# Causal masks added by VectorE, head outputs split in pairs, rotated queries moved by transfers, in a two-layer decoder trunk

## The reference, cut to what matters

```python
D_MODEL = 1024; SEQ = 512; DEPTH = 2          # batch 1
HEAD_DIM = 64; N_HEADS = 16; NSA_GROUPS = 4   # 4 query heads share one key/value group

def nsa_mixer(x, ...):                        # layer 0
    q, kc, vc, ks, vs, kw, vw, gl = split(x @ w_in)
    gates = sigmoid(gl + b_gate)              # three gates for each head and token
    q_rot, k_slc, k_win = apply_rope(q), apply_rope(ks), apply_rope(kw)
    k_cmp, v_cmp = compress(kc, ...), compress(vc, ...)      # 31 compressed keys per group
    # compressed branch: unrotated q, key n seen if 16 n + 31 <= t; rows that see none give 0
    # selected branch: n_sel = min(16, 8) = 8 of 8 blocks, so all of the causal keys
    # window branch: the last 512 positions, so all of the causal keys too
    return (g0 * softmax(q k_cmp) v_cmp + g1 * softmax(q_rot k_slc) v_slc
            + g2 * softmax(q_rot k_win) v_win) @ w_o

def fox_mixer(x, ...):                        # layer 1
    q, k, v, fl = split(x @ w_in)
    cum = cumsum(log_sigmoid(fl + b_f))
    return softmax_causal(q k / 8 + cum_q - cum_k) v @ w_o

def conv_ffn(x, ...):
    h = causal_conv3(x @ w_up) + conv_b
    a, b = split(h)
    return (gelu(a) * b) @ w_down

for i in range(2):
    x = layer_norm(ALPHA * x + mixer_i(x))
    x = layer_norm(ALPHA * x + conv_ffn(x))
```

## Time and profile before

| | us |
|---|---|
| median of 3 runs (lowest, highest) | 1415.19 (1414.56, 1415.60) |
| profiled execution, its own time | 1415.75 |
| its span, first to last instruction | 1414.0 |
| TensorE (PE) busy | 1355.5 |
| VectorE (DVE) busy | 700.9 |
| ScalarE (ACT) busy | 671.1 |
| GpSimd (POOL) busy | 618.3 |

### The profile page before, as it was taken

One profiled execution on the slowest core, in us unless ns is written; L12 is line 12 of the kernel. 1 busy time (PEld: TensorE's weight loads), 2 busy tenths in 40 slices (PEclk: granted clock), 3 DMA queues, 4 the chain that ended last, 5 costly groups with the idle time before them and its releaser, 6 DMA issues.

```text
span 1414.0 us, 20012 instructions
## 1 busy us (share of the span) xinstructions
PE 1355.5 (96%) x7050; PEld 1116.4 (79%) x7050; DVE 700.9 (50%) x1312; ACT 671.1 (47%) x1249; POOL 618.3 (44%) x406
## 2 busy tenths in 40 slices
PE   8979999988999999999999999998999999999997
PEld 6867787867888888888888778877788888888886
DVE  3347777786554434340007578778374343432006
ACT  4347777776234444442213667777234444443110
POOL 2257777673345444444434222223235444444441
PEclk9989999999999999999999999999999999999999
DMA  9432222111333333333232221222423333334221
GB/s 286 100 75 53 45 60 61 54 38 48 124 96 106 97 96 91 102 100 129 99 89 92 69 75 47 66 72 75 149 60 105 104 93 100 89 104 134 91 74 59
DMA packets 170237, 127.59 MB, mean 90 GB/s; under 512 B 24032, under 2 KB 155860, under 8 KB 170164
## 3 DMA queue, kind: packets, MB, share of 16 engines
q1 hardware_dynamic: 170164, 126.63, 30.5%
HBM read 116.98 MB, written 4.39 MB: 86 GB/s over the span
## 4 chain that ended last, share of the span: by engine, by line
PE 78%; DVE 13%; issue 3%; ACT 3%; POOL 2%; DMA 1%; SPq 1%; DVEq 0%; POOLq 0%; ACTq 0%
PE ps L927 15%; PE ps L929 15%; PE ps L928 15%; PE ps L1185 7%; PE ps L1187 6%; PE ps L1184 6%; PE ps L1089 2%; DVE xt L1606 2%; PE ps L1103 2%; PE ps L1056 2%; DVE prob L1463 1%; DVE xt L1596 1%; DVE negmax L1450 1%; DVE stats L1600 1%; PE ps L1225 1%
## 5 line engine op out<-in xcount | busy, mean ns | idle before, releaser
L466 POOL TENSOR_TENSOR wl<-raw,wh 128x1024 fp32r<-128x1024 f32 x178 | 432.7, 2434 | 667.7 <-ACT wh L585 667.6
L927 PE MATMUL ps<-xh,wh 128*128 128x512 f32 x968 | 392.2, 405 | 1.6 <-ACT work L657 1.0
L929 PE MATMUL ps<-xh,wl 128*128 128x512 f32 x968 | 378.9, 391 | 0.0
L928 PE MATMUL ps<-xl,wh 128*128 128x512 f32 x968 | 378.0, 391 | 0.0
L585 ACT ACTIVATE wh<-raw 128x1024 fp32r<-128x1024 f32 x192 | 201.9, 1052 | 201.1 <-PE ps L1187 190.9
L929 PEld LDWEIGHTS ps<-xh,wl 128*128 128x128 f32 x968 | 182.2, 188 | 39.1
L927 PEld LDWEIGHTS ps<-xh,wh 128*128 128x128 f32 x968 | 184.1, 190 | 34.7 <-ACT work L657 1.4
L928 PEld LDWEIGHTS ps<-xl,wh 128*128 128x128 f32 x968 | 182.9, 189 | 32.1
L1627 DVE SCALAR_TENSOR_TENSOR work<-ps,conv,work 128x511 f32<-128x511 f32 x88 | 66.0, 750 | 221.2 <-ACT work L807 155.8
L1596 DVE SCALAR_TENSOR_TENSOR xt<-xt,ps 128x512 f32<-128x512 f32 x32 | 20.5, 682 | 242.7 <-PE ps L1187 242.4
L1185 PE MATMUL ps<-wl,gh 128*128 128x512 f32 x352 | 139.6, 396 | 0.0
(11 more groups left out here) (198 smaller groups left out, 2076.6 us busy)
## 6 DMA issues: line engine op xcount, KB each, us to landing
raw<-in_ffn_w_up SPq DMA_DIRECT2D x88, 512.0 KB, 3.8
raw<-in_ffn_w_down SPq DMA_DIRECT2D x44, 512.0 KB, 3.5
raw<-in_fox_w_in SPq DMA_DIRECT2D x24, 512.0 KB, 4.0
raw<-in_nsa_w_in SPq DMA_DIRECT2D x12, 512.0 KB, 5.5
xt<-in_x SPq DMA_DIRECT2D x8, 512.0 KB, 4.8
raw<-in_nsa_w_in SPq DMA_DIRECT2D x16, 256.0 KB, 3.9
raw<-in_nsa_w_o SPq DMA_DIRECT2D x8, 512.0 KB, 3.8
raw<-in_fox_w_o SPq DMA_DIRECT2D x8, 512.0 KB, 3.5
```

The costliest lines, as they stand in the source:

```text
L466: nc.gpsimd.tensor_tensor(wl[:, slot, :, :], raw[:, slot, :, :], wh[:, slot, :, :].bitcast(F32), ALU.subtract).then_inc(s_wl, 1)
L927: nc.tensor.matmul(o, ah, bh, start=start, stop=False)
L928: nc.tensor.matmul(o, ah, bl, start=False, stop=False)
L929: return nc.tensor.matmul(o, al, bh, start=False, stop=stop)
```

## The change

- The bf16 mask product is gone. `unit_max` is now one instruction that adds the scores (PSUM) and a bf16 tile `seen` [128, 512] (zeros, then the triangle), writes the negated sum to `prob` and accumulates the minimum, which is the negated maximum. It is followed by an instruction that reads the accumulator out. ScalarE takes the exponential from `prob` with scale -1, in place, and no longer from PSUM; TensorE's wait for a free bank of scores is now for that VectorE instruction.
- `head_add` puts two heads into the two halves of `head_sum`, and `heads_hi` and `heads_lo` split 128 partitions once for two heads: 16 of each in place of 32. The copied half goes to `extra`, or to `swapped` in layer 1.
- The hi part of a query item goes to `swapped` and its lo part to `rot2`, each as one operation of 128 partitions. Four transfers of 64 partitions (`move_queries`) take them to `qs`. The next swap and the next sine product wait for them, and so does TensorE before the first scores that use them.
- The sine product stands at w = 1 in place of 2, ScalarE's hi part of queries at w = 2 in place of 3.
- Two small VectorE floors in the compressed branch are gone (L1493, L1502). Before the units begin, the gates of the first 128 tokens are multiplied once by 0 for tokens without a compressed key. `pcs` has one buffer in place of two.

```diff
-            def mask(bank, i, stop=True):
-                return nc.tensor.matmul(ps[:, bank, i * P:(i + 1) * P], identb[:, :], causalb[:, :], start=False, stop=stop)
             def nsa_scores(u):
...
                     pe.wait_ge(s_pl, 4 * g + 3 + h // 2)
+                    pe.wait_ge(s_qm, 64 * (2 * g + 1 + h // 2))
...
                 if u >= 2:
-                    pe.wait_ge(s_ex, u - 1)
+                    pe.wait_ge(s_nm, u - 1)
                 for part in range(2):
-                    nc.tensor.matmul(..., start=part == 0, stop=False)
-                mask(b, i).then_inc(s_sc, 1)
+                    last = nc.tensor.matmul(..., start=part == 0, stop=part == 1)
+                last.then_inc(s_sc, 1)
...
             def unit_max(u, i):
                 dve.wait_ge(s_sc, u + 1)
-                nc.vector.tensor_reduce(negmax[:, u % 4:u % 4 + 1], ps[:, BS + u % 2, 0:(i + 1) * P], AX.X, ALU.max, negate=True).then_inc(s_nm, 1)
+                if u >= 3:
+                    dve.wait_ge(s_pt, u - 2)
+                n = (i + 1) * P
+                nc.vector.tensor_tensor_reduce(out=prob[:, u % 3, 0:n], in0=ps[:, BS + u % 2, 0:n], in1=seen[:, SEQ - n:SEQ], scale=-1.0, scalar=3e38,
+                                               op0=ALU.add, op1=ALU.min, accum_out=negmax[:, u % 4:u % 4 + 1]).then_inc(s_nm, 1)
...
             def unit_exp(u, i):
                 act.wait_ge(s_nm, u + 1)
-                if u >= 3:
-                    act.wait_ge(s_pt, u - 2)
-                nc.scalar.activation(prob[:, u % 3, 0:n], ps[:, BS + u % 2, 0:n], ACT.Exp,
-                                     bias=negmax[:, b:b + 1], accum_out=psumrow[:, b:b + 1]).then_inc(s_ex, 1)
+                nc.scalar.activation(prob[:, u % 3, 0:n], prob[:, u % 3, 0:n], ACT.Exp,
+                                     bias=negmax[:, b:b + 1], scale=-1.0, accum_out=psumrow[:, b:b + 1]).then_inc(s_ex, 1)
...
+            def move_queries(n):
+                q = qs[n // 4 % 2]
+                a = 2 * (n % 4 - 2)
+                sp.wait_ge(s_ph, n + 1)
+                for h, rows in enumerate(halves):
+                    sp.dma_start(q[rows, a + h, :].bitcast(F32), swapped[rows, :]).then_inc(s_qm, 16)
+                sp.wait_ge(s_pl, n + 1)
+                for h, rows in enumerate(halves):
+                    sp.dma_start(q[halves[1 - h], a + h, :].bitcast(F32), rot2[rows, :]).then_inc(s_qm, 16)
             def item_moves(n):
+                if n % 4 == 3 or n % 4 == 0 and n:
+                    move_queries(n - 1)
...
             def item_hi(g, k):
                     act.wait_ge(s_r3, n - (n + 2) // 4 + 1)
+                    if k:
+                        nc.scalar.activation(swapped.bitcast(F32R), rot1, ACT.Copy).then_inc(s_ph, 1)
+                        return
...
-                    if turned and w == (5 if item[1] == 1 else 3):
+                    if turned and w == (3, 5, 2, 2)[item[1]]:
                         item_hi(*item)
...
-                    if turned and w == (6 if item[1] == 1 else 2):
+                    if turned and w == (6 if item[1] == 1 else 1):
                         item_dve(*item)
...
             def head_add(n, bank):
-                nc.vector.tensor_tensor(head_sum[HD:P, :], ps[0:HD, bank, :], head_sum[0:HD, :], ALU.add).then_inc(s_os, 1)
+                x = extra if n < HEADS else swapped[0:HD, :]
+                nc.vector.tensor_tensor(head_sum[n % 2 * HD:(n % 2 + 1) * HD, :], ps[0:HD, bank, :], x[:, :], ALU.add).then_inc(s_os, 1)
-            def head_lo(n, o_h, o_l):
+            def heads_lo(n, o_h, o_l):
                 dve.wait_ge(s_oh, n + 1)
-                at = (slice(n % 2 * HD, (n % 2 + 1) * HD), n % HEADS // 2, slice(None))
-                nc.vector.tensor_tensor(o_l[at], head_sum[HD:P, :], o_h[at].bitcast(F32), ALU.subtract).then_inc(s_ol, 1)
+                nc.vector.tensor_tensor(o_l[:, n % KB, :], head_sum, o_h[:, n % KB, :].bitcast(F32), ALU.subtract).then_inc(s_ol, 1)
```

More of the change, by code:

```diff
@@ L49 @@
 NEG = -1e30
-FLOOR = -1e28
 R = 4
@@ L531, in _ @@
                     rope_sum(0, n)
-                    for h in range(2):
+                    for h in range(1 if n else 2):
                         rope_lo(0, n, h)
```

126 lines of the change are left out of this document (66 added, 60 removed).

## The result

The changed kernel takes 1390.26 us in the median of 4 runs (1387.11 to 1391.82), the kernel before on the same chip 1415.39 (1414.56 to 1416.51): ratio 0.9821, 95% interval 0.9802 to 0.984. The forecast was 1397, range 1386 to 1410: a gain of 18 us was forecast and 25 came. The profiled execution took 1391.82 us, span 1390.0.

A forecast was written before the change was run, and what follows sets the result against it. TensorE, busy 1355.5 of 1414.0 us, was taken as the bound. Groups 0 to 2 -12.5 + 4.0, group 3 -1.5, layer 1 -7.3 and -0.3, start -0.5: -18.1 us, so 1397, range 1386 to 1410.

The forecast's parts named there:

- The mask's price beside its neighbours: TensorE's score stream: each mask product costs 0.13 us by distances of starts, 25.0 us for 192 masks.
- It is on the path where TensorE is the bound: groups 0 to 2 and pairs 0 to 6: Mask time comes off the end there: 12.5 us in groups 0 to 2, 7.3 in pairs 0 to 6 of layer 1.
- What the other engines lose: Units: ScalarE's lost operations gain 0; VectorE at 1.65 us a unit still fits the 1.90 us stage.
- The rotation one unit earlier: Layer 0 units: earlier sine product adds stalls, 0.4 us reaching TensorE at 10 items, 4.0 us lost, bounds 0 to 12.
- The masked maximum: VectorE in the units: main part near 483 ns, added accumulator read 0.16 us, hidden by TensorE's work.
- The transfers: Queries moved by transfers at three group borders: TensorE waits 0.4 in place of 0.56 us, counted 0, bounds -0.5 and +2 each.
- Before the first unit: Start: scores later by 0.7 us, first maximum's product about 1.5 earlier; 0.5 us gain, bounds -1 and +2.
- Group 3 and the last pair: Group 3 of layer 0 gains 1.5 us, bounds 0 and 4.2; the last pair of layer 1 gains 0.3.
- Rival 1: All mask time comes back and the rotation's waits are covered: -26.5 us, 1389 us; chance 0.17.
- Rival 2: The rotation eats layer 0's gain, 1.2 us at each of 10 items: -8 us, 1407 us; chance 0.18.
- rival 3: VectorE becomes the bound in layer 0 through a slower masked maximum: +21 us, 1437 us; chance 0.08.
- Rival 4: The mask was cheap: wide spacing behind it stays, only 0.04 us of issue goes: -3 us, 1412 us; chance 0.05.

The follow-up runs named there:

- the zero product: Changed kernel with a bf16 product of 128 columns, adding zeros, put back where each mask stood: 1393.66 us, ratio 0.9845.
- B: Kernel before with only the paired heads (hi and lo parts once for two heads, one buffer of pcs): 1407.45 us, ratio 0.9936.
- C: Kernel before with only the rotated queries moved by transfers, sine product at w = 1, hi part at w = 2: 1409.33 us, ratio 0.9953.
- D: Kernel before with only the gates of rows without compressed keys zeroed once and the floors gone: 1405.55 us, ratio 0.9925.
- A: Kernel before with only the masks moved from TensorE to the masked maximum on VectorE: 1409.7 us, ratio 0.9957.
- the old places: Changed kernel with the queries' sine product and ScalarE's hi part one unit later, as before, transfers kept: 1387.76 us, ratio 0.9799.

## Why the prediction was right, and where its steps were wrong

The end came out at 1390 where 1397 was forecast. That it lies inside the range is in good part luck: of the gain of 18 us nearly all was to come from TensorE's masks, which gave much less, and the work taken from the other engines, which stood in the sum as nothing, gave more than the masks fell short.

**The mask's price beside its neighbours: right.** From the last score product to the second projection product it was 0.47 to 0.59 us before and is 0.36 to 0.46 now (medians over the units of groups 0 to 2): 0.12 to 0.13 less, and 0.07 less in the units of one tile. In the changed kernel's timeline of TensorE the first projection product behind two score products starts 0.28 and 0.24 us ahead of the next, in place of 0.32, and is followed like any other:

```profile
195.30 0.42 PE L1082 MATMUL ps<-ks,qs 128*128 128x128 f32 x2
195.55 0.44 PE L955 MATMUL ps<-xh,wh 128*128 128x512 f32 x1
195.83 0.39 PE L956 MATMUL ps<-xl,wh 128*128 128x512 f32 x1
...
200.19 0.40 PE L955 MATMUL ps<-xh,wh 128*128 128x512 f32 x1
200.43 0.39 PE L956 MATMUL ps<-xl,wh 128*128 128x512 f32 x1
```

**"It is on the path where TensorE is the bound: groups 0 to 2 and pairs 0 to 6": this step failed.** For groups 0 to 2, 12.5 us were counted. The masks alone gave 3.5 there, leaving them out altogether 5.0, and the zero product in the changed kernel cost 3.1. I had read 61.8 of 65 us busy as "TensorE is the bound"; it was the bound only as long as it was no faster. The waits of the earlier trace rows were a sign: three different releasers came last by turns. How close behind TensorE they came at the other units no row shows. Removing all masks from the kernel before moved its idle time in layer 0 from 20.4 to 24.5 us. In layer 1 there are fewer such operations, and 7.3 forecast stands against 5.2 measured, 4.9 with the masks alone, 3.7 by the zero product: 0.07 to 0.09 us for each of 56 masks. Of the 5.2 and the 4.9 some 0.5 to 1.2 are the clock's: the kernel before had 3.4 us more at the lower one, and kernels with the same code in these pairs differ by so much when their clocks differ so. By the Trainium skill ("TensorE: Matmul & The Clock Gate", section "Back-to-back issue gap") it would be 3.1 with the 56 ns of a product by itself, which the prediction took, and 4.5 with the 81 ns that the section gives for products of 128 columns in a stream with their weight loads. These rows lie near the second, and below my 0.13.

**What the other engines lose was taken at nothing, and gave most of the gain.** The prediction says of ScalarE "it is not the bound at 48 of 65 us, so 0", of VectorE "it still fits", and costs the floors only ahead of the first unit. Alone, up to the first norm, B gave 2.8 us, C 8.8 and D 10.0. With A's 3.2 that makes 24.8, and the change has 16.1 there, 19.9 with the old places: the parts overlap. That each frees the same waits is the likely reason, and about 2 us of C's and of D's figure are the same shorter stretch at the lower clock. The mean load of an engine over a group doesn't tell what stands in the units in which its extra operations lie.

**The rotation one unit earlier: right.** Forecast 4.0 us with a third of each stall reaching TensorE; the stalls are 12.8 us, and 3.7 of them reach the end of the stretch, 2.5 in the medians. Here the clock is alike: both executions have the same 6.8 us at the lower level in group 3.

**The masked maximum: right in its main part**, 484 ns; the read is 82 ns. That it is hidden held in the changed kernel, where leaving it out gives nothing; on the kernel before it cost 3.4 us.

**The transfers.** At the three borders 0 was taken, and TensorE waits 1.9 us in all, where it had waited 1.7 (5.4 less the 3.7 before the first unit). The gain of 4.9 us that the transfers bring was in the sum as nothing. I put it down to the single hi and lo operations that they make possible, but giving half of these back cost nothing, so the cause is open. Before the first unit the scores were forecast 0.7 us later and came 1.1 later: TensorE waits 4.7 us for the transfer in place of 3.7 for GpSimd. One execution each doesn't settle the 1.1, as kernels without transfers start these scores between 90.7 and 92.2 us. What the first maximum won behind them lies inside group 0 and isn't told apart.

**Group 3 and the last pair.** Group 3: 1.9 against 1.5, a hit by two errors. The sum took four lo parts of heads off VectorE there where the change takes off two, so it gets 5.1 us more and only some 2.6 less; and the clock, which cost some 1 to 2 us there, was in no term. The last pair and its projection: 2.4 against 0.3. With B alone this stretch takes 45.6 us in place of 50.0, with C or A alone 50, so it is B's; with B in it, it is 45.5 in some kernels and 47.6 in others, for which I have no cause.

**The rivals.** None came true as told. Rival 1 has the right time, 1389, nearer than the forecast, for a wrong reason: it wanted all of the mask time back. Rival 2 is out by the 2.5 to 3.7 us that the place costs, rival 3 by the masked maximum's 484 ns. Rival 4, the cheap mask, was nearest to the masks' own worth (5.8 us alone), but its reason, that the wide spacing stays, is refuted by the timeline.

**What stays open:** which of the waits each microsecond of B, C and D went through; what the transfers gain by; how much of D is addresses and how much the clock, and whether D's place or its chain counted; and the 2 us that come and go in the last pair.

## What to carry to other kernels

An engine that is 96% busy need not be what a saving comes off: look at what its waits name, and if several engines release it by turns, expect that a saving on it turns into waiting for them. Look for small operations in the stretch in which an in-order engine carries its extra work, also if it is half idle in the mean; taking away 16 operations on 8 columns (with what went with it, clock and addresses) gave 10.4 us here, moving 192 matrix products to another engine 5.8. Cut a compound change into its parts: here the part that the change seemed to be about gave no more by itself than any other. And before a stretch of one trace is held against another's, compare their granted clocks.

## What the runs showed of the hardware

- With all buffers behind one moved by 128 bytes, the down projection's products take 389 in place of 395 ns, 2.6 us for each FFN. One pair of layouts, in which nothing else that I know of differs for them; that the address is the cause was not tested by itself.
- A short VectorE operation with two SBUF inputs took 0.6 us where it met GpSimd's scaling and 0.2 elsewhere (0.58 and 0.20 in the means), and when it was removed, the meeting moved to the next one (0.20 to 0.59).
- The full clock came back sooner in the kernels in which TensorE was busier: around the first units it was at 1.2 GHz for 10.2 us in the four kernels with neither C nor D (TensorE busy for 3.9 of the first 6.8 us in the kernel before), and for 6.8 us or less in the ten others (5.4 with D alone).
- The clock can fall in the middle of the units. In the changed kernel's profiled execution a stretch of group 3 was granted 0.50, which is 1.2 GHz in place of 2.4, after 7.4 us in which TensorE was busy for 4.9. Windows of the two:

```profile
277.00:284.40 7.40, 4.90 (x35) 4.11 (x34) 5.54 (x19) 4.18 (x12) 4.29 (x6) 1.00 0.36 107
284.40:291.20 6.80, 5.89 (x20) 4.57 (x21) 4.35 (x15) 5.36 (x14) 5.36 (x7) 0.50 0.33 77
```

  The records have 20 products in those 6.8 us, and 43 in the next 6.8. Group 3 with its projection took 81.1 us here, and 79.0 in the kernel with the zero product and 80.2 in the one without C, which had no such stretch; this cost was in no term of the prediction. It isn't bound to the faster kernels: those two did without it, and B alone had 3.4 us of it. Of the changed kernel's four runs the two with a mean granted clock of 0.990 took 1391.8 us, those with 0.993 and 0.994 1388.7 and 1387.1; in other kernels the runs show no such order.
